# Rotation tables of an S5 scan: half angles on ScalarE and products on VectorE in place of GpSimd

## What is computed

```python
mag = jnp.exp(lam_re * step)
ab_re = mag * jnp.cos(lam_im * step)
ab_im = mag * jnp.sin(lam_im * step)
...
bu_re = jnp.einsum('blgc,gnc->blgn', uf, bb_re)
bu_im = jnp.einsum('blgc,gnc->blgn', uf, bb_im)
...
pw_re, pw_im, h_re, h_im = lax.associative_scan(
    cplx_affine_combine, (a_re, a_im, bu_re, bu_im), axis=1)
...
y = jnp.einsum('gcn,blgn->blgc', c_re, h_re) - jnp.einsum('gcn,blgn->blgc', c_im, h_im)
```

## Time and profile before

| | |
|---|---|
| Median of 3 runs | 1642.18 us (1638.2 to 1643.94) |
| Profiled execution, own time | 1642.27 us |
| Its span | 1640.6 us |
| Mean granted TensorE clock | 0.973 |
| Busy: TensorE, VectorE, ScalarE, GpSimd | 93%, 43%, 20%, 13% of the span |
| The chain that ended last | TensorE 28%, issue 10%, VectorE 3% of the span |

### The profile page before, as it was taken

The page is one execution under the profiler, slowest core; times in us unless marked ns, Lnnn a source line. Parts: engine busy times, 40 slices in busy tenths (PEclk is TensorE's granted clock), DMA queues, the critical chain, the costliest instruction groups (busy, mean ns, idle before and its releaser), DMA issues. The chain is left out here.

```text
span 1640.6 us, 20665 instructions
## 1 busy us (share of the span) xinstructions
PE 1528.3 (93%) x8124; PEld 1073.0 (65%) x8124; DVE 712.3 (43%) x1768; ACT 327.1 (20%) x852; POOL 207.2 (13%) x305
## 2 busy tenths in 40 slices
PE   6999998999989788999999799979999999999996
PEld 4888886777767666888887467755454445445433
DVE  3546419999974643000243301141343433434336
ACT  3121110111013222111111211123122212212213
POOL 1110116566520000011000000010000000000001
PEclk9999999999999889999999899989999999999998
DMA  9744432434342547443576873625999999999992
GB/s 260 233 143 142 156 130 82 137 128 140 116 139 75 161 133 263 162 141 116 166 251 229 305 237 115 244 104 218 405 402 402 380 403 402 383 401 403 399 405 90
DMA packets 203568, 377.25 MB, mean 230 GB/s; under 512 B 25059, under 2 KB 158479, under 8 KB 178498
## 3 DMA queue, kind: packets, MB, share of 16 engines
q1 hardware_dynamic: 198810, 371.67, 62.1%
q10 hardware_dynamic: 4664, 4.28, 0.8%
HBM read 364.49 MB, written 11.54 MB: 229 GB/s over the span
## 5 line engine op out<-in xcount | busy, mean ns | idle before, releaser
L934 PE MATMUL ps<-ring,M 128*128 128x256 f32 x1024 | 236.2, 387 | 1.6 <-ACT M L947 1.6
L2402 PE MATMUL ps<-ring,M 128*64 128x512 f32 x1024 | 223.3, 594 | 0.4 <-ACT M L2563 0.4
L934 PEld LDWEIGHTS ps<-ring,M 128*128 128x128 f32 x1024 | 193.5, 193 | 39.0 <-issue 13.9
L645 PE MATMUL ps<-X,ring 128*128 128x264 f32 x896 | 204.7, 390 | 0.0
L645 PEld LDWEIGHTS ps<-X,ring 128*128 128x128 f32 x896 | 170.5, 192 | 29.4 <-issue 0.4
L2402 PEld LDWEIGHTS ps<-ring,M 128*64 128x64 f32 x1024 | 72.2, 137 | 137.8 <-issue 137.0
L315 PE MATMUL ps<-SH,ring 128*128 128x264 f32 x512 | 116.1, 391 | 6.4 <-PEq L1515 6.4
L1816 PE MATMUL ps<-X,ring 128*128 128x264 f32 x512 | 117.7, 386 | 1.6 <-PEq L1566 1.6
L2255 PE MATMUL ps<-X,ring 128*128 128x264 f32 x512 | 118.7, 392 | 0.0
L2460 PE MATMUL ps<-SH,M 128*64 128x512 f32 x512 | 113.4, 595 | 1.3 <-DVE XT L2840 1.3
L315 PEld LDWEIGHTS ps<-SH,ring 128*128 128x128 f32 x512 | 98.6, 193 | 23.9 <-issue 6.8
(11 more groups left out here) (486 smaller groups left out, 1772.8 us busy)
## 6 DMA issues: line engine op xcount, KB each, us to landing
SH<-in_moe_w_down SPq DMA_DIRECT2D x32, 2048.0 KB, 12.1
ring<-in_moe_w_gate SPq DMA_DIRECT2D x64, 1024.0 KB, 11.9
ring<-in_moe_w_up SPq DMA_DIRECT2D x64, 1024.0 KB, 14.3
ring<-in_w_in SPq DMA_DIRECT2D x14, 2048.0 KB, 8.6
ring<-in_xa_wk SPq DMA_DIRECT2D x8, 2048.0 KB, 8.9
ring<-in_xa_wv SPq DMA_DIRECT2D x8, 2048.0 KB, 9.1
ring<-in_w_out SPq DMA_DIRECT2D x8, 2048.0 KB, 8.2
ring<-in_xa_wq SPq DMA_DIRECT2D x8, 2048.0 KB, 8.1
```

Of the source, the lines that this page charges most:

```text
L645: mm = nc.tensor.matmul(ps[:, n % 4, 0:T], w[:, d, o * P:(o + 1) * P], xn[:, d, :], start=(d == 0), stop=(d == KB - 1))
L934: mm = nc.tensor.matmul(ps[:, kv_bank(s), a * 256:(a + 1) * 256], memT[:, k, a * P:(a + 1) * P], w[:, k, :], start=(k == 0), stop=(k == KB ...
L2402: mm = nc.tensor.matmul(ps[64 * e:64 * e + 64, 0, :], xg[:, p % 3, k, e, :], gate_up_unit(e, half)[:, :, k % 8, :], start=(k == 0), stop=( ...
```

## The change

GpSimd has no instructions left in the second block. The first block keeps only the angles, in turns between a half and minus a half (`turns`); the quarter turn and the two sines are gone. For every step VectorE adds high and low angles to 256 sums (`angle_sum`). ScalarE takes of each sum the absolute value, the sine of half the angle, the cosine of half the angle (as a sine of the rest to a quarter turn), the doubled square of the half sine, and one minus that, which is the cosine. VectorE multiplies half sine and half cosine to half of the sine (`sine`), and the two products that use it (L1078, L1090) become instructions with a factor of 2. The half sine and half cosine have one buffer each: ScalarE writes them again when VectorE has multiplied them. ScalarE's stream is written anew: in the first two chunks of a pair stand the half angles of the step after next, the state copies of the present step and the cosine, ahead of the slab and key copies of that place; the Silus of z come in the last pair.

```diff
@@ first block, VectorE
-                st(v.tensor_tensor(sinT, per_e(high), entries, ALU.mult))
-                st(wrap(sinT, cosT))
-                st(v.tensor_tensor(cosT, per_e(turn), entries, ALU.mult))
-                st(v.tensor_tensor(sinT, sinT, cosT, ALU.add))
-                st(wrap(sinT, cosT))
-                st(v.tensor_scalar(cosT, sinT, 0.25, None, ALU.add))
-                dve.wait_ge(wide_ready.sem, wide_ready.at(4))
-                wrap(cosT, tabtmp).then_inc(angle_ready.sem, angle_ready.up())
+                st(v.tensor_tensor(turns, per_e(high), entries, ALU.mult))
+                st(wrap(turns, turn_tmp))
+                st(v.tensor_tensor(turn_tmp, per_e(turn), entries, ALU.mult))
+                st(v.tensor_tensor(turns, turns, turn_tmp, ALU.add))
+                wrap(turns, turn_tmp)
@@ first block, ScalarE
-                    elif n == 9:
-                        act.wait_ge(wide_ready.sem, wide_ready.at(8))
-                        act.wait_ge(angle_ready.sem, angle_ready.at(2))
-                        nc.scalar.activation(sinT, sinT, ACT.Sin, scale=TWO_PI, bias=eps_c[:, 1:2]).then_inc(sine_ready.sem, sine_ready.up())
-                        nc.scalar.activation(cosT, cosT, ACT.Sin, scale=TWO_PI, bias=eps_c[:, 1:2]).then_inc(sine_ready.sem, sine_ready.up())
@@ first block, GpSimd
+                st(gp.memset(eps_c[:, 2:3], 0.5 * PI))
@@ second block
+        angle = X[:, 3072:3584].rearrange("p (s t) -> p s t", s=2)
+        half_sin, half_cos = X[:, 3584:3840], X[:, 3840:4096]
-            @block.gpsimd
-            def _(pool):
...
-                    tt(cos, hi(cosT), lo(cosT), ALU.mult)
-                    tt(sin, hi(sinT), lo(cosT), ALU.mult)
-                    st(tt(tmp, hi(sinT), lo(sinT), ALU.mult))
-                    st(tt(cos, cos, tmp, ALU.subtract))
-                    st(tt(tmp, hi(cosT), lo(sinT), ALU.mult))
-                    tt(sin, sin, tmp, ALU.add).then_inc(rot_ready.sem, rot_ready.up())
@@ second block, VectorE
+                def angle_sum(t):
+                    hi = turns[:, t, 16:32].unsqueeze(2).to_broadcast([P, 16, 16])
+                    lo = turns[:, t, 0:16].unsqueeze(1).to_broadcast([P, 16, 16])
+                    tt(square(angle[:, t % 2, :]), hi, lo, ALU.add).then_inc(angle_ready.sem, angle_ready.up())
+
+                def sine(t):
+                    dve.wait_ge(half_ready.sem, half_ready.at(3 * t + 3))
+                    tt(W[:, t % 2, 1, :], half_sin, half_cos, ALU.mult).then_inc(rot_ready.sem, rot_ready.up())
+                    if t + 2 < NT:
+                        angle_sum(t + 2)
+
+                angle_sum(0)
+                angle_sum(1)
                 tt(both(carried), both(s5h[:, :, :, :]), every_b(AR, 16), ALU.mult)
...
+                sine(0)
                 for t in range(NT):
...
+                    dve.wait_ge(cos_ready.sem, cos_ready.at(2 * t + 2))
                     dve.wait_ge(rot_ready.sem, rot_ready.at(t + 1))
...
-                    tt(by_sin, bu[:, :, 0:TP], sin, ALU.mult)
+                    stt(by_sin, bu[:, :, 0:TP], 2.0, sin, ALU.mult, ALU.mult)
...
-                    tt(by_sin, gsc, sin, ALU.mult).then_inc(rot_used.sem, rot_used.up())
+                    stt(by_sin, gsc, 2.0, sin, ALU.mult, ALU.mult).then_inc(rot_used.sem, rot_used.up())
...
+                    if t + 1 < NT:
+                        sine(t + 1)
@@ second block, ScalarE
-                for k in range(8):
-                    nc.scalar.activation(z[:, k, :], z[:, k, :], ACT.Silu)
+                def half_angles(t):
+                    act.wait_ge(angle_ready.sem, angle_ready.at(t + 1))
+                    if t:
+                        act.wait_ge(rot_ready.sem, rot_ready.at(t))
+                    nc.scalar.activation(half_cos, angle[:, t % 2, :], ACT.Abs).then_inc(half_ready.sem, half_ready.up())
+                    nc.scalar.activation(half_sin, angle[:, t % 2, :], ACT.Sin, scale=PI,
+                                         bias=eps_c[:, 1:2]).then_inc(half_ready.sem, half_ready.up())
+                    act.wait_ge(half_ready.sem, half_ready.at(3 * t + 2))
+                    nc.scalar.activation(half_cos, half_cos, ACT.Sin, scale=-PI,
+                                         bias=eps_c[:, 2:3]).then_inc(half_ready.sem, half_ready.up())
+
+                def cosine(t):
+                    cos = W[:, t % 2, 0, :]
+                    if t >= 2:
+                        act.wait_ge(rot_used.sem, rot_used.at(t - 1))
+                    nc.scalar.activation(cos, half_sin, ACT.Square, scale=ROOT2).then_inc(cos_ready.sem, cos_ready.up())
+                    act.wait_ge(cos_ready.sem, cos_ready.at(2 * t + 1))
+                    nc.scalar.activation(cos, cos, ACT.Copy, scale=-1.0, bias=1.0).then_inc(
+                        cos_ready.sem, cos_ready.up())
+
+                for t in range(2):
+                    half_angles(t)
+                    cosine(t)
                 for p in range(NT // 2):
 
                     for c in range(3):
                         j = 3 * p + c
+                        if c < 2:
+                            t = 2 * p + c
+                            if t + 2 < NT:
+                                half_angles(t + 2)
+                                copy_states(t)
+                                cosine(t + 2)
+                            else:
+                                if t + 2 == NT:
+                                    for k in range(8):
+                                        nc.scalar.activation(z[:, k, :], z[:, k, :], ACT.Silu)
+                                copy_states(t)
                         if j % 4 == 3:
                             take_kv(act, j // 4)
                         if j >= 4 and j % 4 == 0 and j // 4 <= 8:
                             take_keys(j // 4 - 1)
-                        if c == 1 and p:
-                            copy_states(2 * p - 2)
-                            copy_states(2 * p - 1)
-                copy_states(30)
-                copy_states(31)
```

More of the change, by code:

```diff
@@ L34 @@
 TWO_PI = 6.2831850
+PI = 3.1415925
+ROOT2 = 1.4142135
 INV_2PI = 0.15915494309189535
@@ L127, in build @@
         work = sb("work", [P, 4240])
-        eps_c = sb("eps_c", [P, 2])
+        eps_c = sb("eps_c", [P, 3])
         ps = ctx.enter_context(nc.psum_tensor("ps", [P, 8, 512], F32))
@@ L405, in build @@
         bwide = A[:, 2048:4096].rearrange("p (i t a c) -> p i t a c", i=2, a=2, c=16)
-        tabtmp = A[:, 0:1024].rearrange("p (t e) -> p t e", e=32)
         BT = S[:, 0:2048].rearrange("p (i q n) -> p i q n", i=2, q=8)
         CT = S[:, 2048:4096].rearrange("p (i q n) -> p i q n", i=2, q=8)
-        cosT = S[:, 4096:5120].rearrange("p (t e) -> p t e", e=32)
-        sinT = S[:, 5120:6144].rearrange("p (t e) -> p t e", e=32)
+        turn_tmp = S[:, 4096:5120].rearrange("p (t e) -> p t e", e=32)
+        turns = S[:, 5120:6144].rearrange("p (t e) -> p t e", e=32)
         MAG, TURN, COR, COI, AR, AI, NAI = range(7)
@@ L914, in build @@
                                 "s5_states_ready", "s5_states_copied", "s5_outputs_done", "s5_output_block_taken"))
+        angle_ready, half_ready, cos_ready = (signal(s) for s in ("angle_sum_ready", "half_angle_ready", "cosine_ready"))
         NT = 32
@@ L1058, in _ @@
                 both = lambda x: x.rearrange("p i b t -> p (i b) t")
+                square = lambda a: a.rearrange("p (a b) -> p a b", a=16)
+                def angle_sum(t):
[9 more added lines that the diff above has]
+                angle_sum(1)
                 tt(both(carried), both(s5h[:, :, :, :]), every_b(AR, 16), ALU.mult)
@@ L1508, in build @@
                        s5_tr, s5_trt, kv_taken, keys_tr, keys_tr_taken, kv_stored, rot_ready, rot_used, bu_done,
-                       bu_taken, state_ready, state_copied, y_done, y_taken))
+                       bu_taken, state_ready, state_copied, y_done, y_taken, angle_ready,
+                       half_ready, cos_ready))
         sig = A[:, 0:8 * T].rearrange("p (k t) -> p k t", t=T)
```

## The result

| | before | changed |
|---|---|---|
| Median | 1640.26 us of 4 runs (1638.2 to 1643.94) | 1618.88 us of 4 runs (1617.9 to 1620.63) |
| Profiled execution, its span | 1642.27, 1640.6 | 1620.63, 1618.4 |
| Granted TensorE clock, mean | 0.973 | 0.976 |

Over every run of this study the kernel before has a median of 1640.0 us in 30 runs (1636.71 to 1643.94) and the changed one 1619.2 in 10 (1617.58 to 1622.13).

A forecast was written before the change was run, and what follows sets the result against it. VectorE, slowed by GpSimd beside it, paced the scan pairs while TensorE waited. Returned waits of 12.6 us (18.57 less 6.0) plus 2.3 of clock made 14.9, from 1642.27 to 1627.4 us; range 1623 to 1637.

The forecast's parts named there:

- (a): GpSimd leaves the scan stage: a VectorE step running alone takes 5.18 us, with GpSimd beside it 7.17.
- (b): Two VectorE products become scalar_tensor_tensor over 512 elements: 0.05 us dearer each, 0.10 a step, at most 0.28 each.
- (c): VectorE gains a sine product and an angle sum each step: step 6.30 us, upper end 7.1.
- (d): A pair of scan steps takes VectorE 12.85 us, just under TensorE's 12.93, so TensorE paces and its per-pair wait goes.
- (e): ScalarE gains five activations of 256 elements, some 2.6 us of scan work a step; VectorE does not wait for them.
- (f): Key/value copies queue on ScalarE behind the scan work: TensorE's transposes get new waits of 1.5 and 0.95 us.
- (g): Start of the scan: step 0 at 247.8 us after a table load; TensorE's first wait falls from 6.25 to 3.6.
- (h): Silus of z move to the last pair, covered by TensorE's tail; work saved in the stage before returns nothing.
- Dear products: Rival: the 512-element products keep VectorE nearer 6.9 us a step; time 1635 us, chance 0.08.
- reloaded tables: Rival: Sin and Abs or Square need different tables, so ScalarE reloads twice a step; 1637 us, chance 0.06.
- another engine takes GpSimd's place: Rival: ScalarE's SBUF work or another cause keeps VectorE's instructions at 0.84 us; step 7.75, time 1657 us, chance 0.08.
- the gain is lost later: Rival: a later stage bound by transfers that began at their own time swallows the gain; 1641 us, chance 0.08.

## Why the prediction was right and wrong

**What bounded the kernel, and (a): right.** The kernel with GpSimd's work taken away and the one with it put back show the same from both sides: beside GpSimd VectorE's instructions of 256 elements with two SBUF inputs go from 0.42 to 0.84 us, without it they stay at 0.42, and TensorE then paces.

**(b), dearer products: wrong, by 0.10 us a step.** The nearest row was of another size, and the addition taken from it does not exist: 0.680 us against 0.684 for the plain product beside it (L1070). The upper bound, twice 0.477 less 0.69, is 0.26 and not 0.28; nothing hangs on it.

**(c), the step: right in kind.** 5.18 + 3 x 0.34 = 6.20, and 6.18 was measured; the 6.30 of the prediction is this and the 0.10 of (b).

**(d): right.** The pairs go at TensorE's 12.85 us, and the kernels with one and four more products lie where the limit of some 6.6 us a step puts them.

**(e): right.** The Sins take 0.493 and 0.508 us, Abs, Square and Copy 0.40 to 0.42. In the changed kernel's scan VectorE has no wait for ScalarE, not even at the start.

**(f): right in kind, too dear by 1.0 us.** The two waits are where they were put, 1.13 and 0.29 us where 1.5 and 0.95 were reckoned. Both hang on the end of an early step of VectorE, and every step came sooner than forecast.

**(g), the start: this step failed.** It counted a table load of 1.28 us, put step 0 at 247.8, which is 4.0 us after the block's start, and left a first wait of 3.6 (255.6 less 252.06 is 3.5). There is no load, and step 0 came 3.5 us after the start; with a load put there it came after 4.0, as reckoned. The table of the Silus served Sin and Abs too. No row of the kernel before showed that; it showed the other order, Silus after the Sins of the earlier trace rows, with a load of their own:

```profile
145.92 1.28 ACT L870 ACT_TABLE_LOAD   x1
```

The banks of pair 1 were free 11.1 us after the start, where 11.8 were reckoned: 0.5 from the load and 0.2 from the shorter step and its hand-over. That is 0.7 of the 2.4 us by which the first wait, 1.17, fell short of 3.6. The other 1.7 is the fall of the clock at the block's start, which brought TensorE to this wait later.

**(h): right** for the first block, whose TensorE is still full, and for the Silus, which took 2.6 us with nobody behind them.

**The sum: three of its steps failed.** The first is the term "waits left: 3.6 + 1.5 + 0.95 = 6.0", which measured 1.17 + 1.13 + 0.29 = 2.59. Of the difference, 0.7 is (g), 1.0 is (f), and 1.7 is the fall at the block's start, which only moves time from the wait to the clock.

The second is the clock. The 2.3 returned was met in size, but by luck: the fall that was left in, behind the first wait, did not come, and the one that came, at the block's start, costs nothing by itself, as the kernel before shows. Put in its own terms, the scan gave back 0.7 + 1.0 + 1.7 and 0.4 of smaller gaps more than forecast: 18.7 where 14.9 stood.

The third is what lies outside the scan. With 18.7 the sum from 1642.27 comes to 1623.6, still in the range, and 1618.88 was measured. The prediction began at one execution, and the 30 runs of the kernel before have a median of 1640.0: 2.3 of the rest. The medians over all runs differ by 20.8 and the scans by 18.7 to 20.4, so some 0.4 to 2 us more lie outside the scan, to which the prediction gave nothing. The profiles point to the block behind; whether by chance or by the change is open. The lower end of the range, 1623, stood only 2.7 below the best case that was reckoned (1625.7), where the runs of the kernel before alone are up to 7 us apart.

**The rivals.** Dear products and reloaded tables fall by the rows above: in the scan no load stands at all. The Trainium skill (ScalarE: Activation LUTs, Table sets: the hidden batching unit) has abs in every set; the trace agrees, and shows more, as Sin too ran on the table loaded for Silu here. Of the 2.66 us that the Trainium skill (ScalarE: Activation LUTs, What ACT_TABLE_LOAD costs) gives for a switch, the kernel with the load shows 1.283, with Sin 0.02 us behind it. That another engine takes GpSimd's place falls: ScalarE was busy for 93.44 us of the scan, and L1086 is at 0.42 in every step. That the gain is lost later falls as well: the span is shorter by more than the scan.

## What to carry to other kernels

When two identical instructions of one engine take 0.42 and 0.84 us, look for the engine that runs beside the slow one before cutting work: moving the tables here gave VectorE more to do and less time to do it in. Then reckon the step at which the next engine takes over the pace (here 6.6 us); what is well below it is free, and what stays are the waits of the start and of whatever is queued behind the new work. And look at the same kernel's profile several times before a gain or a loss of 2 us outside the changed stage is put down to the change.

## What was not expected of the hardware

- The table loaded for Silu served Sin, Abs, Square and Copy too: in the changed kernel there is none between the load at 144.9 us and the block behind the scan. The converse does not hold: where a table had been loaded for Sin (244.15 us, in the kernel with the load at the start), the Silus behind it had a load of their own at 444.63.
- A VectorE instruction with a factor and two operands over 512 elements took 0.680 us, as long as a product without the factor.
- The contention goes both ways and sorts by operands: with two SBUF inputs 0.83 to 0.84 us in place of 0.42, with one from PSUM 0.68 unchanged, and GpSimd's own products 0.79 to 0.80 beside them.
- A fall of the clock ahead of a wait cost nothing: 32 products took 8.86 us and not 7.17, the wait behind them 4.57 and not 6.25, and what followed began 14.5 us after the start in both executions. Behind the last wait of the scan the same 8.86 made the scan 240.06 us long and not 238.6.
- The block behind the scan took 98.3 to 105.6 us in executions of the two kernels with the same instructions, at granted clocks of 0.95 to 0.88.
